# State-space outputs of a hybrid decoder step: two group pairs at a time, on the lower and the upper half of the PSUM partitions

## What is computed

```python
xr = jnp.einsum('btgc,gpc->btgp', uf, bbr)
xi = jnp.einsum('btgc,gpc->btgp', uf, bbi)
...
_, _, hr, hi = lax.associative_scan(_cplx_affine_combine, (a_r, a_i, xr, xi), axis=1)
...
y = (jnp.einsum('btgp,gcp->btgc', hr, c_re) - jnp.einsum('btgp,gcp->btgc', hi, c_im)
     + d_skip.reshape(SSM_NGROUPS, SSM_GROUP) * uf)
```

## Time and profile before

| | |
|---|---|
| time, median of 3 runs | 2208.56 us (2201.27 to 2213.98) |
| span of the profiled execution | 2206.9 us, 1.7 us below the median (of its time, this is what is given) |
| TensorE busy | 2091.7 us (95%) |
| weight loads / VectorE / ScalarE / GpSimd busy | 1952.5 / 1070.8 / 806.2 / 112.5 us |
| outputs of the eight parts, with what lies between them | 437.9 to 546.4 us of the span |

### The profile page before, as it was taken

How to read it: one execution, slowest core, us unless ns; L and a number is a source line. 1 busy time by engine, 2 the same in 40 slices (tenths; PEclk the granted TensorE clock), 3 DMA queues, 4 the chain that set the end, 5 groups by cost and what they waited for, 6 DMA issues and landing times.

```text
span 2206.9 us, 39164 instructions
## 1 busy us (share of the span) xinstructions
PE 2091.7 (95%) x15964; PEld 1952.5 (88%) x15964; DVE 1070.8 (49%) x1725; ACT 806.2 (37%) x1164; POOL 112.5 (5%) x168
## 2 busy tenths in 40 slices
PE   8999898898899788899999999999999999999997
PEld 6999787787898455589999999999999999999996
DVE  4343487853465344464564444444444444444443
ACT  5222232243244355574433433323332333233344
POOL 1000011000000121200001000000000000000011
PEclk9999899999897899999999999999999999999999
DMA  7645543443455888855655455455445554555443
GB/s 179 200 133 152 134 129 102 112 117 94 119 164 212 323 326 324 304 178 163 197 179 152 134 153 152 137 162 154 145 134 154 161 152 134 144 160 151 146 132 114
DMA packets 552965, 364.75 MB, mean 165 GB/s; under 512 B 64737, under 2 KB 528050, under 8 KB 552018
## 3 DMA queue, kind: packets, MB, share of 16 engines
q1 hardware_dynamic: 471042, 314.00, 46.3%
q10 hardware_dynamic: 80096, 41.25, 7.0%
q0 software_dynamic: 1712, 7.97, 1.0%
HBM read 345.45 MB, written 23.63 MB: 167 GB/s over the span
## 4 chain that ended last, share of the span: by engine, by line
PE 55%; issue 7%; SPq 1%; DMA 1%; DVE 1%; ACT 1%; POOL 1%; POOLq 0%; DVEq 0%; ACTq 0%
PE bank L279 54%; SPq L1277 1%; SPq L1278 1%; POOL ysT L1726 0%; DMA arena<-in_cache_kv_dram 0%; DMA xT<-out_dram 0%; DVE w_lo L255 0%; PE bank L1859 0%; PE bank L1834 0%; ACT w_hi L250 0%; PE bank L2075 0%; POOL arena L1736 0%; DVE rstd L2589 0%; PE bank L1793 0%; ACT xT L2328 0%
## 5 line engine op out<-in xcount | busy, mean ns | idle before, releaser
L279 PE MATMUL bank<-hx,w_hi 128*128 128x320 f32 x3072 | 676.3, 309 | 1.5 <-DVE w_lo L255 1.5
L255 DVE TENSOR_TENSOR w_lo<-w_raw,w_hi 128x2048 fp32r<-128x2048 f32 (+2 forms) x222 | 463.9, 2089 | 348.3 <-ACT w_hi L250 348.2
L279 PE MATMUL bank<-act,w_hi 128*128 128x320 f32 x2432 | 537.0, 310 | 3.2 <-DVE w_lo L255 2.4
L279 PEld LDWEIGHTS bank<-hx,w_hi 128*128 128x128 f32 x3072 | 513.5, 188 | 2.0 <-issue 1.8
L250 ACT CAST w_hi<-w_raw 128x2048 fp32r<-128x2048 f32 (+2 forms) x222 | 385.6, 1737 | 319.7 <-PE bank L279 317.7
L279 PE MATMUL bank<-hx,w_lo 128*128 128x320 f32 x1536 | 474.6, 309 | 0.0
L279 PEld LDWEIGHTS bank<-act,w_hi 128*128 128x128 f32 x2432 | 405.6, 188 | 4.6 <-DVE w_lo L255 3.1
L279 PE MATMUL bank<-act,w_lo 128*128 128x320 f32 x1216 | 375.8, 309 | 0.0
L279 PEld LDWEIGHTS bank<-hx,w_lo 128*128 128x128 f32 x1536 | 288.4, 188 | 0.0
L662 PE MATMUL bank<-actr,half_hi 128*128 128x320 f32 x1024 | 241.4, 325 | 19.3 <-DVE half_lo L633 19.2
L279 PEld LDWEIGHTS bank<-act,w_lo 128*128 128x128 f32 x1216 | 228.3, 188 | 0.0
(11 more groups left out here) (396 smaller groups left out, 1846.3 us busy)
## 6 DMA issues: line engine op xcount, KB each, us to landing
arena<-in_cache_kv_dram SPq DMA_DIRECT2D x120, 512.0 KB, 6.6
w_raw<-in_w_gate_dram SPq DMA_DIRECT2D x44, 1024.0 KB, 5.2
w_raw<-in_w_up_dram SPq DMA_DIRECT2D x44, 1024.0 KB, 5.2
w_raw<-in_w_down_dram SPq DMA_DIRECT2D x64, 704.0 KB, 4.6
half_raw<-in_w_in_dram ACTq DMA_DIRECT2D x64, 512.0 KB, 4.1
w_raw<-in_w_in_dram SPq DMA_DIRECT2D x20, 1024.0 KB, 5.1
w_raw<-in_w_glu_dram SPq DMA_DIRECT2D x32, 512.0 KB, 4.9
w_raw<-in_w_out_dram SPq DMA_DIRECT2D x16, 1024.0 KB, 5.8
```

Of the source, the lines that this page charges most:

```text
L255: nc.vector.tensor_tensor(w_lo[s][:, 0:job.kt * job.width], raw[s][:, 0:job.kt * job.width], w_hi[s][:, 0:job.kt * job.width].bitcast(F32) ...
L279: mm = pe.matmul(bank[:, 0:NT], w[s][:, at:at + P], x[:, kk, :], start=first and k == 0 and m == 0, stop=final and k == job.kt - 1 and m == 2)
```

## The change

TensorE makes two pairs of a part at a time: pairs u and u + 2, "side" 0 and 1. Side 0 has its results at PSUM partitions 0 to 39, side 1 at 64 to 103 of the same bank, and the products of the two sides alternate. ScalarE copies both with one instruction of 104 partitions (the 24 in between hold nothing of use). `urows` then holds a side's two pairs in 64 columns, and a part is stored with two DMAs, each of 40 partitions in pieces of 256 bytes. The counts of `y_full` and `y_copied` go from four to two for a part, those of `y_stored` from 16 to 32.

```diff
@@ SP, spread_g (L792)
-                        sp.wait_ge(S("y_full"), PG * (part - 1))
+                        sp.wait_ge(S("y_full"), 2 * (part - 1))
@@ SP, stores (L802)
-                    sp.wait_ge(S("y_copied"), PG * (part + 1))
-                    sp.dma_start(y_dram.rearrange("(a s) c -> a s c", s=L)[:, :, part * PG * 32:(part + 1) * PG * 32],
-                                 urows[part % 2][0:NCH, :, :]).then_inc(S(f"y_stored{part % 2}"), 16)
+                    sp.wait_ge(S("y_copied"), 2 * (part + 1))
+                    for side in range(2):
+                        col = (part * PG + 2 * side) * 32
+                        sp.dma_start(y_dram.rearrange("(a s) c -> a s c", s=L)[:, :, col:col + 64],
+                                     urows[part % 2][64 * side:64 * side + NCH, :, 0:64]).then_inc(S(f"y_stored{part % 2}"), 16)
@@ TensorE, outputs_of (L936)
-                    for i in range(PG):
-                        n = part * PG + i
+                    for u in range(2):
+                        n = 2 * part + u
                         if n >= 2:
 
                             pe.wait_ge(S("y_copied"), n - 1)
-                        out = [PS[4 + 2 * (n % 2) + h][0:NCH, 0:P] for h in range(2)]
+                        out = [[PS[4 + 2 * u + h][64 * side:64 * side + NCH, 0:P] for side in range(2)] for h in range(2)]
                         for h in range(2):
-                            pe.matmul(out[h], UTa[:, n, h * NCH:(h + 1) * NCH], Tt[part % 2][:, h, i, :], start=True, stop=False)
+                            for side in range(2):
+                                i = 2 * side + u
+                                pe.matmul(out[h][side], UTa[:, part * PG + i, h * NCH:(h + 1) * NCH], Tt[part % 2][:, h, i, :],
+                                          start=True, stop=False)
                         for r in range(2):
-                            for h in range(2):
-                                rows = slice(h * 64, (h + 1) * 64)
-                                mm = pe.matmul(out[h], Ha[rows, :, r, n], Q[part % 2][rows, r, i, 1:L + 1, :].rearrange("p k c -> p (k c)"),
-                                               start=False, stop=r == 1)
+                            for side in range(2):
+                                i = 2 * side + u
+                                for h in range(2):
+                                    rows = slice(h * 64, (h + 1) * 64)
+                                    mm = pe.matmul(out[h][side], Ha[rows, :, r, part * PG + i],
+                                                   Q[part % 2][rows, r, i, 1:L + 1, :].rearrange("p k c -> p (k c)"), start=False, stop=r == 1)
                         mm.then_inc(S("y_full"), 1)
@@ ScalarE, copies (L1030)
-                        act.wait_ge(S(f"y_stored{part % 2}"), 16 * (part // 2))
-                    for i in range(PG):
-                        n = part * PG + i
-                        act.wait_ge(S("y_full"), n + 1)
+                        act.wait_ge(S(f"y_stored{part % 2}"), 32 * (part // 2))
+                    for u in range(2):
+                        act.wait_ge(S("y_full"), 2 * part + u + 1)
                         for h in range(2):
-                            ins = nc.scalar.copy(urows[part % 2][0:NCH, :, i * 32 + h * CH:i * 32 + (h + 1) * CH],
-                                                 PS[4 + 2 * (n % 2) + h][0:NCH, 0:P].rearrange("p (s c) -> p s c", s=L))
+                            ins = nc.scalar.copy(urows[part % 2][0:64 + NCH, :, u * 32 + h * CH:u * 32 + (h + 1) * CH],
+                                                 PS[4 + 2 * u + h][0:64 + NCH, 0:P].rearrange("p (s c) -> p s c", s=L))
```

More of the change, by code:

```diff
@@ L1175, in make_q @@
                     if part >= 2:
-                        dve.wait_ge(S("y_full"), PG * (part - 1))
+                        dve.wait_ge(S("y_full"), 2 * (part - 1))
                     V.tensor_tensor(q[:, 0], rows(0), spread(PK[:, 0]), ALU.mult)
@@ L1695, in _ @@
                 for b in range(2):
-                    sp.wait_ge(S(f"y_stored{b}"), 16 * (NPART // 2))
+                    sp.wait_ge(S(f"y_stored{b}"), 32 * (NPART // 2))
                 page_done(0)
```

## The result

| | before | changed |
|---|---|---|
| time, median | 2207.51 us (2201.11 to 2213.98, 6 runs) | 2196.03 us (2190.8 to 2198.48, 6 runs) |
| ratio to before | | 0.9941, 95% interval 0.9918 to 0.9964 |
| span of the profiled execution | 2206.9 us | 2189.0 us |
| mean granted clock of TensorE over the span | 0.974 | 0.981 |
| outputs of part 0 to the last dense work of the stage | 437.92 to 542.74: 104.8 us | 437.41 to 532.23: 94.8 us |

Of the profiled execution's 17.9 us, **10.0 come from the stage that was changed**, 0.5 from ahead of it, and 7.4 from behind it.

What follows compares the result with a forecast made beforehand. TensorE bounds the kernel (busy 2091.7 of 2206.9 us); with the change SP's queue caps parts at 12.84 us. The stage's 11.4 us less 0.4 give 11.0: span 2195.9, median 1.7 higher, forecast 2197.5 us, range 2190 to 2207.

Steps and rivals of the forecast that it cites:

- two pairs, both sides at once: TensorE's outputs: 0.57 us for the 128-row run plus 0.61 for the 64-row run, 1.18 in all.
- taps(2) after the start of part 0's outputs: First part: VectorE is busy with the scan's end, so taps(2) start only 1.28 us earlier, at 448.61.
- a spread: SP's queue: the 16 DMAs of a part's spread take about 11.1 us of SP's time.
- parts apart: Cadence of the parts: SP's queue by itself, one spread and two stores with gaps, 12.84 us.
- The open point: 64-row products: four array quarters work at once, 0.59 us plus 0.02 for staggered starts; no row showed it.
- rival 1: 64-row products: only two quarters at once, 0.98 us for a run; −8.7 us, 2199.9 us; chance 0.12.
- Rivals 2 and 3: Outputs: halves don't overlap, 0, 2208.6 us, chance 0.05; each alternation of side drains the array, +7.3, 2215.9 us, chance 0.04.
- The cap: Cadence: SP's queue becomes the longest, so 1.6 of the 2.27 us saved in each part come through.
- The sentence on the slack: SP's queue: from taps to possible outputs 15.9 us against TensorE's 16.9, so SP's slack is 1.0 us.
- Rivals 4 and 5: SP's store issues: 1.78 us each, −1.9, 2206.7 us, chance 0.09; 0.4 us each, −11.8, 2196.8 us, chance 0.12.
- The term that was off: Stage end: outputs(7) start at 529.0 and the dense work at 531.4 instead of 542.74, 11.4 us less.
- the 0.4 us taken off for the queue's waits: SP's queue: allowance for waits between two issues that no row shows, bringing 11.4 us down to 11.0.

Runs made afterwards that it cites:

- e1: The change, with the spread of a part in 8 DMAs instead of 16; 2189.7 us, 0.993 of the kernel before the change.
- e3: The change, with y of a part stored by four DMAs in 128-byte pieces instead of two in 256-byte ones; 2201.4 us, 0.9982 of the kernel before.
- e6: The change without the alternation: in each run all products of one side first, then the other's; 2193.5 us (one run).
- e8: The change, plus spread in 8 DMAs, ScalarE's rounding ahead of the copies, and four pairs in one run; 2181.8 us, 0.988 of the kernel before.
- e5: The change's order of products, but all results on one half, partitions 0 to 39; 2204.5 us (one run).
- e10: The change, with the two stores of a part issued by ScalarE between its two D() instead of by SP; 2193.6 us, 0.9936 of the kernel before.

## Why the prediction was right

| step of the prediction | forecast | measured |
|---|---|---|
| two pairs, both sides at once | 1.18 us | 1.20 |
| outputs of a part | 2.36 | 2.39 |
| taps(2) after the start of part 0's outputs | 10.69 (11.97 − 1.28) | 10.84 |
| a store's issue of 256-byte pieces | 0.81, two 1.66 with the gap | 1.64 for two |
| a spread | 11.1 | 10.75 to 11.36 |
| parts apart | 12.84 | 12.81, mean of parts 2 to 7 |
| what comes off | 11.0 | 10.0 in the stage |
| time | 2197.5 | 2196.0 |

- **The products.** L1881 and L1802 were the right rows to go by the earlier trace rows. The open point, four quarters for 64-row products, came out as I took it, and rival 1 (two at a time, 0.98 us for a run) is refuted by 0.63 us. Rivals 2 and 3 are out with it.
- **The cap.** That over 2 us were saved for each part on TensorE and only 1.65 (14.46 − 12.81) would come through was the main claim. e1 and e3 show it from both sides.
- **The sentence on the slack** doesn't hold as it stands. The prediction gives SP a slack of 1.0 us in bold, and its working is that of the landing of `Tt`. SP's queue itself was busy for 11.1 + 0.85 = 12.0 of 14.46 us and stood idle for the rest (2.2 us ahead of spread(3)). The cap follows from the round that the prediction adds up under the cadence, 12.84 us with two stores: 14.46 − 12.84 = 1.6. So the forecast doesn't hang on the 1.0 us, and no run tests them.
- **The stores.** 0.82 us each with the gap, as one of 512-byte pieces took: the number of pieces is the same. Rivals 4 and 5 are out. The rule of the Trainium skill on transfers under 512 bytes ("DMA: Bandwidth & Descriptors", the table at the top) left no mark here; nobody waits for them in any run, so their landing stays unmeasured.
- **The term that was off** is the last: outputs(7) and the end of the stage. The prediction had them wait for `Tt` and then take 2.36 us. It did not ask what 3.3 us of idleness do to the clock: they took 3.70. Those 1.3 us more than cover the difference between the forecast −11.0 and the stage's −10.0; the 0.4 us taken off for the queue's waits hide the rest of them. The kernel before waited 1.5 us there and kept its clock.
- **The time** agrees better than the stage does (−11.5 against −10.0). That is luck: the runs' scatter, and no merit of the working.

## What to carry to other kernels

When a fast engine is relieved, work out at once how long the next loop is that passes through it: here a queue that was busy for 12.0 us of a round of 14.5, and took 6.8 of 16.8 us. A DMA's issue costs its queue 0.6 to 0.8 us for 16 to 320 pieces, so the number of DMAs in a loop is a cost of its own. Put small results on both halves of the result partitions, in any order of the two (e6), and group products of the same shape (e8). And where a wait of TensorE grows, count the clock behind it as well.

## What the runs showed of the hardware that I had not expected

**Four quarters of the array run at once** with float32 products of 64 rows and 40 columns: 16 passes in 0.63 us, where two quarters took 1.03 (e5), and with the sides in turn the overlap stays (e6). The forecast took this without a row that showed it.

**The issue of a DMA is priced by the DMA.** A spread of 8 DMAs with twice the pieces each took 5.8 to 6.3 us, one of 16 took 10.8 to 11.4 in the change. Stores of 320 pieces took about 0.8 us each with 512, 256 and 128 bytes for a piece (0.81 for one, 1.64 for two, 3.21 for four).

**Idleness can cost twice, and its length alone doesn't tell.** After 3.3 us without work TensorE came back at the lower clock, in the change. In e10 the waits ahead of parts 2 and 4 are alike, 1.58 and 1.59 us in the rows above, and the first is followed by products at the full clock (L944 in 0.64 us), the second by the lower one. The window of part 4's outputs, with a granted clock of 0.56:

```profile
490.10:494.00 3.90, 3.83 (x49) 2.50 (x49) 0.00 (x0) 0.43 (x2) 0.00 (x0) 0.56 0.16 38
```

In e3 a wait of 2.17 us was harmless, too. In the kernel before, one of 1.50 was the earlier trace rows. And the lower clock can come later than the work: in e3, after the wait of 1.99 us, L950 still took 0.64 us, and L957 took 1.11 from 494.61 on (rows above), so part 4's outputs took 2.92 us instead of 2.39. What else decides wasn't tried.

**The scatter of the runs goes with the clock, elsewhere.** Behind the stage the profiled execution of the change took 1656.8 us (532.2 to 2189.0) and that of before 1664.2 (542.7 to 2206.9), with the same program. One and the same instruction of GpSimd starts 10.5 us earlier in the change at the start of that stretch (545.38 against 555.89), 17.9 us earlier at 933.61 (951.52), and 17.9 us earlier at the end, too. Windows of 467.8 us from the end of the stage on, changed and then before:

```profile
532.20:1000.00 467.80, 410.47 (x4328) 315.97 (x4325) 227.84 (x542) 224.51 (x458) 54.30 (x58) 0.95 0.67 239
```

```profile
542.70:1010.50 467.80, 416.08 (x4235) 320.52 (x4233) 223.03 (x536) 222.09 (x455) 52.30 (x58) 0.92 0.67 239
```

The granted clock is 0.95 in one and 0.92 in the other, and the faster one got 93 passes further. So the 7.4 us lie in this window; that the clock is their cause fits the rows, and no run shows it. e8's remainder is 1659.7 us, e10's 1655.2: it varies from one execution to the next, whatever the kernel. So for an edit of this size a stage of the trace is the better measure, and the time of a few runs can, by an estimate from these remainders (1655.2 to 1664.2 us), give it some 5 us too much or too little. What sets these phases of the lower clock wasn't tried.
